# Second block's global attention scores as high and low products; the gated total and the causal layers' filling moved

## The reference

```python
def global_attn(q, k, v, ck, cv):
    k_all = jnp.concatenate([ck, k], axis=1)      # 256 context keys and 512 own keys
    v_all = jnp.concatenate([cv, v], axis=1)
    ...
    o = lax.map(lambda qblk: dense_attn(qblk, k_all, v_all), qb)
```

## Time and profile before

| what | us |
|---|---|
| median of 3 runs (lowest, highest) | 2295.92 (2295.89, 2296.02) |
| the profiled execution | 2296.61 |
| its span in the trace | 2294.8 |
| PE busy in the span | 2281.1 (99%) |
| DVE busy | 1438.1 (63%) |
| ACT busy | 1107.9 (48%) |
| POOL busy | 396.4 (17%) |

### The profile page before, as it was taken

One profiled execution on the slowest core, in us unless ns is written; L12 is line 12 of the kernel. 1 busy time (PEld: TensorE's weight loads), 2 busy tenths in 40 slices (PEclk: granted clock), 3 DMA queues, 4 the chain that ended last, 5 costly groups with the idle time before them and its releaser, 6 DMA issues. The chain is left out here.

```text
span 2294.8 us, 30499 instructions
## 1 busy us (share of the span) xinstructions
PE 2281.1 (99%) x11966; PEld 1885.7 (82%) x11966; DVE 1438.1 (63%) x2318; ACT 1107.9 (48%) x1801; POOL 396.4 (17%) x297
## 2 busy tenths in 40 slices
PE   9999999999999999999999999999999999999998
PEld 8877788888888778888888878888888889888887
DVE  7898569858644666773676475557778335543543
ACT  6666654324434555442444366775555234432442
POOL 0013222202210001220222130001102122220222
PEclk9999999999999999999999999999999999999999
DMA  5222144433423223443343231011112432332231
GB/s 192 74 83 84 56 165 147 165 102 124 150 84 101 93 60 132 157 168 117 110 152 105 85 106 56 11 49 56 56 51 74 129 109 89 111 101 93 92 113 62
DMA packets 70222, 233.05 MB, mean 102 GB/s; under 512 B 8032, under 2 KB 10208, under 8 KB 69952
## 3 DMA queue, kind: packets, MB, share of 16 engines
q1 hardware_dynamic: 70080, 231.11, 30.3%
HBM read 224.18 MB, written 4.28 MB: 100 GB/s over the span
## 5 line engine op out<-in xcount | busy, mean ns | idle before, releaser
L487 PE MATMUL psum<-hH,wH 128*128 128x512 f32 (+1 forms) x1840 | 732.2, 398 | 0.6 <-DVE hL L641 0.3
L489 PE MATMUL psum<-hH,wL 128*128 128x512 f32 (+1 forms) x1840 | 714.6, 388 | 0.0
L488 PE MATMUL psum<-hL,wH 128*128 128x512 f32 (+1 forms) x1840 | 713.8, 388 | 0.0
L474 DVE TENSOR_TENSOR wL<-raw,wH 128x1024 fp32r<-128x1024 f32 (+2 forms) x353 | 446.3, 1264 | 362.1 <-ACT wH L469 361.0
L469 ACT ACTIVATE wH<-raw 128x1024 fp32r<-128x1024 f32 (+2 forms) x353 | 363.5, 1031 | 503.6 <-PE psum L489 476.7
L489 PEld LDWEIGHTS psum<-hH,wL 128*128 128x128 f32 x1840 | 345.3, 188 | 71.3
L487 PEld LDWEIGHTS psum<-hH,wH 128*128 128x128 f32 x1840 | 345.8, 188 | 70.6 <-issue 4.3
L488 PEld LDWEIGHTS psum<-hL,wH 128*128 128x128 f32 x1840 | 346.2, 188 | 61.3 <-issue 0.7
L2030 POOL TENSOR_TENSOR sg<-sg,cv 128x512 f32<-128x512 f32 x66 | 95.1, 1441 | 677.1 <-ACT sg L1857 677.1
L487 PE MATMUL psum<-gH,wH 128*128 128x512 f32 x506 | 197.0, 389 | 0.0
L489 PE MATMUL psum<-gH,wL 128*128 128x512 f32 x506 | 196.9, 389 | 0.0
(11 more groups left out here) (402 smaller groups left out, 3532.1 us busy)
## 6 DMA issues: line engine op xcount, KB each, us to landing
raw<-in_up SPq DMA_DIRECT2D x132, 512.0 KB, 3.2
raw<-in_dn SPq DMA_DIRECT2D x48, 704.0 KB, 4.0
raw<-in_win SPq DMA_DIRECT2D x56, 512.0 KB, 3.3
mbuf<-in_wmod SPq DMA_DIRECT2D x48, 512.0 KB, 3.3
raw<-in_we SPq DMA_DIRECT2D x33, 512.0 KB, 3.4
tm<-toep SPq DMA_DIRECT2D x32, 256.0 KB, 4.3
raw<-in_wo SPq DMA_DIRECT2D x32, 256.0 KB, 2.6
raw<-in_wq SPq DMA_DIRECT2D x16, 512.0 KB, 3.3
```

The lines of the kernel that those rows point to most:

```text
L474: ve.do.tensor_tensor(flat_of(wLb, n), flat_of(rawb, n), flat_of(wHb, n).bitcast(F), ALU.subtract).then_inc(*w_lo.up(n))
L487: pe.do.matmul(o, H[:, k, :], high(k), start=k == 0, stop=False)
L488: pe.do.matmul(o, H[:, k, :], low(k), start=False, stop=False)
L489: ins = pe.do.matmul(o, L[:, k, :], high(k), start=False, stop=k == kt - 1)
```

## The change

Five things change.

1. The global scores. bqT (queries, 4 rows of 512 columns) and bkT (keys, 768 columns) get high parts (bqH, bkH) and low parts (bqL, bkL). A global step's scores become, for each r = 0, 1, 2, the three products bqH*bkH, bqL*bkH, bqH*bkL, each for u = 0 and u = 1 in turn: 18 products of 64 rows by 256 columns in place of 6 fp32 ones. The step's at_b signal (which keeps the two row halves from writing one PSUM bank at the same time) is given after r = 0 and waited for before the first product of r = 2 with u = 0.
2. Who makes the parts: ACT copies to the high part (`ac_global`) behind the second halves of wide steps 11 to 15, in the order query 0, keys, query 1, 2, 3; POOL subtracts (at the end of `po_block2`) in the same order, behind its rotations. bqL and bkL take the places of bqT and bkT themselves; bqH takes the second half of mixed2, bkH lies in XT rows 6 and 7, for which ACT waits until they are parked. PE's global steps wait for the low parts in place of the norm of the context keys.
3. The gated total (`pe_end_sums`) goes from behind the whole second context unit (k = 7) to behind its tile k = 2.
4. C1's filling: two more ticks ahead of the first step, two fewer behind the last.
5. E0's filling: steps 6 and 7 get (4, 3) ticks in place of (3, 3), steps 32 and 33 get (1, 1) in place of (2, 1).

```diff
--- before.py
+++ after.py
@@ -189,6 +189,7 @@
     def turned(x):
         return x.rearrange("p (i n) -> p i n", n=128)[:, :, ::-1]
 
+    xt_at = top[0]
     XT = sb("XT", [128, KD, S])
     hH = sb("hH", [128, KD, S], R)
     hL = sb("hL", [128, KD, S], R)
@@ -279,8 +280,11 @@
     SP = sb("SP", [128, 2, 2, 769])
     PU_at = top[0]
     PU = sb("PU", [128, 12, 128])
+    bq_at = top[0]
     bqT = sb("bqT", [128, 4, S])
     akT, bkT = [sb(f"{x}kT", [128, 768], at=yc_at + 2048 + 3072 * i) for i, x in enumerate("ab")]
+    bqH, bqL = sb("bqH", [128, 4, S], R, at=mark1 + 4 * S * 4), sb("bqL", [128, 4, S], R, at=bq_at)
+    bkH, bkL = sb("bkH", [128, 768], R, at=xt_at + 6 * S * 4), sb("bkL", [128, 768], R, at=yc_at + 2048 + 3072)
     avR, bvR = [[sb(f"{x}{i}", [128, 3, 128], at=tails[2 * (x == "bvR") + i]) for i in range(2)]
                 for x in ("avR", "bvR")]
     band = sb("band", [128, 640])
@@ -819,15 +823,15 @@
     def layer_order(a):
 
         if a.layer == 1:
-            out_ = [("ticks", 64 + 20)]
+            out_ = [("ticks", 64 + 22)]
             per = [(2, 2)] * 28 + [(2, 1)] * 6 + [(0, 0)]
-            last = 10 + 32
+            last = 8 + 32
         else:
             out_ = [("ticks", 58)]
             for n in range(24):
                 out_ += [("ticks", 1), ("index", n), ("ticks", 1)]
             out_.append(("ticks", 2))
-            per = [(4, 3)] * 6 + [(3, 3)] * 18 + [(2, 2)] * 6 + [(2, 1)] * 4 + [(0, 0)]
+            per = [(4, 3)] * 8 + [(3, 3)] * 16 + [(2, 2)] * 6 + [(2, 1)] * 2 + [(1, 1)] * 2 + [(0, 0)]
             last = 2 + 32
         for s, (n, m) in enumerate(per):
             keep = [("keep", 2 if s < 2 else 3)] if a.layer == 0 and s < 18 else []
@@ -1236,10 +1240,23 @@
                 pe.wait_ge(*rp_d.at(("q", g, c)))
                 pe.wait_ge(*rp_d.at(("k", g)))
                 if g:
-                    pe.wait_ge(*hn_x.at("kc"))
+                    pe.wait_ge(*qk_l.at(("global", "k")))
+                    pe.wait_ge(*qk_l.at(("global", c)))
+                    for r in range(3):
+                        for n_, (q_, k_) in enumerate(((bqH, bkH), (bqL, bkH), (bqH, bkL))):
+                            for u in range(2):
+                                blocks, at0, _ = wide_parts(s, u)
+                                r0, b, o = 64 * u, blocks[2 * r], at0 + 256 * r
+                                if u == n_ == 0 and o >= 1536:
+
+                                    pe.wait_ge(*at_b.at(("wide", s)))
+                                ins = pe.do.matmul(psum[:, o:o + 256], q_[r0:r0 + 64, c, i * 128:i * 128 + 128],
+                                                   k_[r0:r0 + 64, b * 128:b * 128 + 256], start=n_ == 0, stop=n_ == 2)
+                        if r == 0:
+                            ins.then_inc(*at_b.up(("wide", s)))
                 else:
                     pe.wait_ge(*ev_a.at((at["win", 4], "ctx")))
-                for u, r in wide_issue(s):
+                for u, r in () if g else wide_issue(s):
                     blocks, at0, runs = wide_parts(s, u)
                     n_, r0 = sum(runs[:r]), 64 * u
                     w_, b, o = 128 * runs[r], blocks[n_], at0 + 128 * n_
@@ -1325,6 +1342,9 @@
                     rotated(ac, key)
                     ac.wait_ge(*rp_c.at(key))
                 ac.do.activation(mixed2[:, 4 * g + c, :], bank[7], ACT.Copy).then_inc(*at_fh.up(("wide", q // 4)))
+            if 11 <= s < 16:
+
+                ac_global(ac, global_parts[s - 11])
             yield
 
     def ve_wide(ve):
@@ -2220,8 +2240,8 @@
                 pe.wait_ge(*x_s.at((("dn1", 1), 7)))
             for k in range(KD):
                 pe_tile(pe, n, c_part(pe, bank[2 * i + 1][:, :CTX]), k)
-            if i == 1:
-                pe_end_sums(pe)
+                if (i, k) == (1, 2):
+                    pe_end_sums(pe)
         for slot in range(KD + 4):
             for i, n in enumerate(ns):
                 if 0 <= slot - 2 * i < KD:
@@ -2363,6 +2383,27 @@
         ffn1_done(po)
         for key in ropes2:
             po_rope(po, key)
+        for key in global_parts:
+            po.wait_ge(*qk_h.at(("global", key)))
+            full, high, low = global_rows(key)
+            po.do.tensor_tensor(low, full, high.bitcast(F), ALU.subtract).then_inc(*qk_l.up(("global", key)))
+
+    global_parts = (0, "k", 1, 2, 3)
+
+    def global_rows(key):
+
+        return (bkT[:], bkH[:], bkL[:]) if key == "k" else (bqT[:, key, :], bqH[:, key, :], bqL[:, key, :])
+
+    def ac_global(ac, key):
+
+        if key == "k":
+            ac.wait_ge(*rp_d.at(("k", 1)))
+            ac.wait_ge(*hn_x.at("kc"))
+            ac.wait_ge(*d_park.at(1))
+        else:
+            ac.wait_ge(*rp_d.at(("q", 1, key)))
+        full, high, _ = global_rows(key)
+        ac.do.activation(high, full, ACT.Copy).then_inc(*qk_h.up(("global", key)))
 
     def sp_block2(sp):
         ffn1_done(sp)
```

## The result

The changed kernel takes 2301.44 us (median of 8 runs, 2301.11 to 2304.48) against 2295.91 (8 runs, 2295.74 to 2296.33): 5.5 us slower, a ratio of 1.0028 with the interval [1.0017, 1.0039]. The forecast was 2288.7, in a range of 2286.8 to 2292.0, and faster. It was wrong in size and in sign.

A forecast was written before the change was run, and what follows sets the result against it. PE, working in 99% of the span, was taken as the bound. Gains of 3.1 (global scores), 2.7 (gated total), 0.8 (E0) and 0.6 (C1) sum to 7.2 us, taking 2295.92 to 2288.7 us; range 2286.8 to 2292.0.

The forecast's parts named there:

- The global scores: Global steps: scores take 1.24 in place of 1.49 us; 4.0 over 16 steps, less 0.9 lost, leaves 3.1 us.
- The waits for DVE's scaling: Global steps, a sign of the forecast: PE's waits on DVE's scaling go up from 0.8 to about 1.7 us.
- The making of the parts: ACT's five copies and POOL's five subtractions for the global scores: cost 0; ACT's delays together 3.3 us if cover fails.
- The rival of the weight loads: Global steps: weight loads pace the pairs, a step takes 2.3 us, the kernel 2304.4 us; chance 0.04.
- The gated total: Between the blocks: total moves 1.80 us earlier; with 1.05 for the clock, less 0.15 of short waits, 2.7 us won.
- the clock's term: Between the blocks: the half-speed stretch goes and the clock stays up, winning 1.05 us, half of 2.1 on PE's path.
- The wait goes just about: 0.8 us: E0, steps 6 and 7: one tick more each removes PE's 0.69 us wait for Pr, winning 0.8 us.
- the wait comes back a step later: E0's lower bound of 0: the removed wait returns a step later, since DVE has no room in the top-k.
- something unseen in the causal layers: Rival in the causal layers: something unseen there costs over 4 us; chance 0.02.
- the last sentence of the prediction: Signs against it: PE waiting for low parts at step 16, late ACT exps in steps 12 to 15, new causal-layer waits.
- I take none: E0, steps 32 and 33: losing the two ticks costs no PE wait, since the trace has none there.
- gets 1.37 us of fill: C1: the 0.6 us wait for the last keys' low part (kLr) is filled, winning 0.6 us; bounds 0 and 0.65.

The follow-up runs named there:

- one tick: Kernel before with E0's filling one tick forward in place of two (step 6 alone at (4, 3), one tick less in step 33): 2297.41 us, ratio 1.0006.
- the heads apart: Changed kernel with both old fillings, each column block of a global step doing head 0's three products first, then head 1's: 2291.29 us.
- a third of the products left out: Changed kernel with both old fillings, the second head's bqL*bkH and bqH*bkL left out, 12 products a global step in place of 18: 2291.31 us.
- without either: Changed kernel with E0's and C1's fillings as in the kernel before, no edit to the global products: 2291.19 us, ratio 0.9979.
- wH and wL back: Kernel before with E0's new filling, but from unit 19 on ACT's wH and DVE's wL made two ticks later: 2297.94 us, ratio 1.0009.

## Why the prediction was wrong, and where it was right

**The global scores: right.** A step of the changed kernel, from its first pair to the next group (timeline of PE):

```profile
1448.00 0.38 PE L1253 MATMUL psum<-bkH,bqH 64*128 64x256 f32 x2
...
1449.25 1.53 PE L1286 MATMUL psum<-PU,bvR 128*64 128x128 f32 x24
```

A pair takes 0.118 (forecast 0.115), coming in and out 0.2, a step 1.26 in place of 1.24. The waits for DVE's scaling went from 0.8 to 1.4 (1.7 forecast): from the start of the last scores to the turning it is 0.82 at the first odd step and 0.67 at the last but one where 0.21 is usual (0.62 and 0.46 before, where 0.31 was usual), and 0.03 more at three others. -3.0 in the trace, -2.9 alone. The making of the parts costs nothing that can be seen. The rival of the weight loads is out: with the loads one behind the other a step would have taken 2.3.

**The gated total: the mechanism right, the clock's term too large.** The first token tiles of the changed kernel (timeline of PE):

```profile
1283.32 0.40 PE L2216 MATMUL psum<-hH,wH 128*128 128x512 f32 x1
...
1284.20 0.50 PE L2216 MATMUL psum<-hH,wH 128*128 128x512 f32 x1
...
1285.64 0.51 PE L2216 MATMUL psum<-hH,wH 128*128 128x512 f32 x1 [0.48 <-DVE hL L2344]
```

On the scale of before (less 10.14) that is 1273.18, 1274.06 and 1275.50; forecast were 1273.2, 1274.05 and 1275.5, and the clock stayed up, as forecast. But the 1.05 for the clock was taken from one profiled execution as if each had it. The fall costs 0.8 and the median of before doesn't have it. The whole gain in the medians is 1.8, near the 1.80 - 0.15 of the waits. That the profiled pair shows 2.6, close to the 2.7 of the sum, is luck in part: the execution of before that was profiled happened to have the fall. The warning was in sight: the profiled execution stood 0.7 above its median, and I carried that difference along as a constant.

**E0: wrong, by 8.5** (+7.7 in the traces where -0.8 was forecast). The wait for Pr in step 7 did go. The step that failed is making a gain of that, "The wait goes just about: 0.8 us", with a lower bound of 0, "the wait comes back a step later". It did come back a step later, as 0.8 at the scores of step 8, and the account stopped there: I had followed the two ticks only to the one place where a wait stood. But the ticks are kept until step 32. Up to step 23 four steps hold 24 ticks, three units of 8 (from step 24 on 16, two units), so each pair of heads meets the filling in the same phase; a shift that changes the order on ACT and DVE changes it for six pairs. I had shown the new order at one place only. The same pattern stands in DVE's list (wL ahead of the minima) at every pair, and there the slack, 1.15, could have been read: 191.72 + 0.81 against 193.68. A rival "the shift repeats, and PE waits at each pair" would have been priced from wH 1.05 + wL 1.22 - 1.15 = 1.1 a pair, for six pairs some 6.7 us, on the slow side (an estimate made afterwards, and too high for the last two pairs, whose wH and wL take 0.62 and 0.68; the five waits that came are between 0.5 and 1.8, 5.0 together, and step 24 has none). It had no place among my rivals, and "something unseen in the causal layers" got a chance of 0.02, though the last sentence of the prediction names just this sign, new waits of the causal layers "whose steps now meet the filling two ticks later". A second term was put at nothing without a price: the ticks taken from steps 32 and 33, for which "I take none". In the changed kernel PE waits 0.73 in step 32 and 0.33 a step earlier; in the run with one tick, which leaves step 32 as it was, it doesn't. No run separates this from the shift.

**C1: wrong, by 3.0.** The wait for kLr did go. The step that failed is taking that for all that the two ticks do, "gets 1.37 us of fill", with bounds of 0 and 0.65: the ticks also move SP's fetch, and that costs a wait of 2.2 for the minimum. SP's queue had no place in the prediction. tm's four loads stood 4.0 ahead of the scores that need them, and the fetch that passed them waits for a wL that DVE makes at 734.85.

**The sum.** In the profiled pair -2.6 - 3.0 + 0.2 + 7.7 + 2.4 = 4.7, the spans differ by 4.8. The medians differ by 5.5, the missing 0.7 being the fall of the clock in the profiled execution of before. The single parts add up to 7.9 + 3.3 - 1.8 - 2.9 = 6.5, 1.0 too much. 0.4 of it is C1, whose wait for the minimum is 2.6 alone and 2.2 behind the slower E0 (by the traces C1 costs 2.8 and 2.4); where the rest lies is open.

## What to carry to other kernels

When filling is moved in a periodic schedule, find the period of both sides first: a shift that isn't taken back is paid at every period, and the place to look is every in-order queue, the DMA queue included, for the instructions that change sides, each with the slack of who waits behind it. The small terms of a change (here 0.8 and 0.6) can carry its largest risks; a term whose gain is one wait needs a lower bound worked out as far as the edit reaches. And a clock fall in one profiled execution is worth its price only if the other executions have it: compare the profiled time with the median first.

## What the runs showed of the hardware

The two halves of TensorE's rows ran their products not only side by side but each in its own sequence, ahead of up to two products issued before them on the other half: 2291.29 with the heads apart, 2291.31 with a third of the products left out, 2291.19 without either. The Trainium skill (TensorE: Matmul & The Clock Gate, Part 3: Packing small matmuls, row/col tiling) has the side-by-side running, and the trace agrees (two products of 256 columns in 0.118); it also says that products keep strictly to the order of issue in their starts, and here the row at 1444.70 stands ahead of the one at 1444.81. The measurement decides.

The granted clock fell to half (1.2 of 2.4 GHz) for 3.4 us in some executions of the same instructions and not in others: between the blocks in the traces of before and of three edited kernels (the scores alone, one tick, wH and wL back), not in five others with the same instructions there; in E0 in the changed kernel's trace behind a wait of 1.83, not in that of its filling alone, with a wait of 1.84 at the same place.
